# Gated DeltaNet in a hybrid layer: diagonal blocks of 16 by substitution on VectorE, and a second product buffer

## The reference

```python
h = rmsnorm(x, pre_norm)
proj = h @ w_in                      # 6.7k columns in three groups
# group a: gated DeltaNet, 4 heads of 128; group b: SSD, 16 heads; group c: retention, 4 heads
x = x + rmsnorm(concat(o_a, o_b, o_c) @ w_out, post_norm)
```

```python
a_low = einsum('bihd,bjhd->bhij', kb, ki) * decay * strict
sol = triangular_solve(a_low + eye, rhs, lower=True)     # then v_new = u - w @ S, and the state S moves on
```

## Time and profile before

| | us |
|---|---|
| median of three runs (2158.16 to 2159.24) | 2159.18 |
| the profiled execution's own time | 2162.2 |
| its span, first to last instruction | 2160.4 |
| PE busy, 14884 matmuls | 2080.1 |
| DVE busy | 1368.3 |
| ACT busy | 888.7 |
| POOL busy | 483.2 |

### The profile page before, as it was taken

One profiled execution on the slowest core, in us unless ns is written; L12 is line 12 of the kernel. 1 busy time (PEld: TensorE's weight loads), 2 busy tenths in 40 slices (PEclk: granted clock), 3 DMA queues, 4 the chain that ended last, 5 costly groups with the idle time before them and its releaser, 6 DMA issues.

```text
span 2160.4 us, 38435 instructions
## 1 busy us (share of the span) xinstructions
PE 2080.1 (96%) x14884; PEld 1918.3 (89%) x14884; DVE 1368.3 (63%) x3012; ACT 888.7 (41%) x1777; POOL 483.2 (22%) x432
## 2 busy tenths in 40 slices
PE   7899999999999999999999998999999999999996
PEld 6687889999898898999988898889988989999995
DVE  5678766646478876534577786774546787745333
ACT  5543366423343426511354445653325333652111
POOL 3433343322000112100333343432300010211000
PEclk9998999999999999999999999999999999999998
DMA  6653556667553455454575546667754343653442
GB/s 240 242 176 117 176 195 234 244 215 283 184 198 106 157 191 180 157 178 164 179 264 186 185 161 242 236 225 254 258 201 174 140 174 130 213 208 114 163 161 97
DMA packets 98196, 410.66 MB, mean 190 GB/s; under 512 B 11168, under 2 KB 12256, under 8 KB 84192
## 3 DMA queue, kind: packets, MB, share of 16 engines
q1 hardware_dynamic: 97440, 407.79, 53.8%
q10 hardware_dynamic: 576, 0.41, 0.1%
HBM read 257.00 MB, written 151.16 MB: 189 GB/s over the span
## 4 chain that ended last, share of the span: by engine, by line
PE 84%; issue 4%; DVE 4%; DMA 4%; ACT 2%; POOL 1%; SPq 0%; POOLq 0%; DVEq 0%; ACTq 0%
PE ps L1301 80%; PE ps L1304 4%; DMA wk<-cum_rows 1%; DMA wo_loaded<-in_w_out 1%; DMA wo_split<-wo_parts 1%; POOL w_low L2357 1%; DVE base L1795 1%; DMA w_split<-w_low 0%; ACT wk L2231 0%; DVE slot L1693 0%; DVE base L1794 0%; DMA wk<-in_x 0%; DMA w_loaded<-in_w_in 0%; DVE acc L2011 0%; DVE wk L1846 0%
## 5 line engine op out<-in xcount | busy, mean ns | idle before, releaser
L1301 PE MATMUL ps<-w_hi,hT_hi 128*128 128x256 f32 x1792 | 529.7, 296 | 11.8 <-POOL w_low L2357 10.0
L1301 PE MATMUL ps<-w_hi,hT_lo 128*128 128x256 f32 x1792 | 504.1, 281 | 0.0
L1301 PE MATMUL ps<-w_low,hT_hi 128*128 128x256 f32 x1792 | 502.9, 281 | 0.0
L2357 POOL TENSOR_TENSOR w_low<-w_loaded,w_hi 128x512 fp32r<-128x512 f32 x208 | 285.7, 1390 | 411.1 <-ACT w_hi L2074 411.0
L1301 PEld LDWEIGHTS ps<-w_hi,hT_hi 128*128 128x128 f32 x1792 | 338.9, 189 | 19.6 <-POOL w_low L2357 11.5
L1301 PEld LDWEIGHTS ps<-w_low,hT_hi 128*128 128x128 f32 x1792 | 339.3, 189 | 5.2 <-issue 4.8
L1301 PEld LDWEIGHTS ps<-w_hi,hT_lo 128*128 128x128 f32 x1792 | 340.2, 190 | 0.0
L1301 PE MATMUL ps<-hT_hi,w_hi 128*128 128x512 f32 x768 | 323.0, 421 | 9.4 <-POOL w_low L2357 9.4
L1301 PE MATMUL ps<-hT_lo,w_hi 128*128 128x512 f32 x768 | 304.2, 396 | 0.0
L1301 PE MATMUL ps<-hT_hi,w_low 128*128 128x512 f32 x768 | 303.8, 396 | 0.0
L1301 PE MATMUL ps<-wo_parts,mixT_hi 128*128 128x256 f32 x960 | 272.0, 283 | 0.0
(11 more groups left out here) (213 smaller groups left out, 3740.5 us busy)
## 6 DMA issues: line engine op xcount, KB each, us to landing
w_loaded<-in_w_in SPq DMA_DIRECT2D x104, 512.0 KB, 5.2
w_split<-w_hi SPq DMA_DIRECT2D x52, 1024.0 KB, 8.2
w_split<-w_low SPq DMA_DIRECT2D x52, 1024.0 KB, 10.1
w_hi<-w_split SPq DMA_DIRECT2D x104, 512.0 KB, 6.3
w_low<-w_split SPq DMA_DIRECT2D x104, 512.0 KB, 7.2
wo_loaded<-in_w_out SPq DMA_DIRECT2D x32, 512.0 KB, 4.4
wk<-cum_rows SPq DMA_DIRECT2D x32, 512.0 KB, 4.5
wo_split<-wo_parts SPq DMA_DIRECT2D x32, 512.0 KB, 8.6
```

The lines of the kernel that those rows point to most:

```text
L1301: return nc.tensor.matmul(o, a, b, start=start, stop=stop)
L2357: tt(w_lo[at], wr[at], w_hi[at], ALU.subtract)\
```

## The change

Blocks are 16 x 16 (`BASE` = 16), so `FIRST` is 4 and three levels are left; there are fifteen columns and sixteen row broadcasts. `COPIES` = 8 broadcasts are held at a time, in the head's own XT buffer: eight are made, four to a part, and used, then the other eight. Two product buffers `aTs` are used in turn by head parity; the new one is the spare quarter of slot 0, which tile 19 (the last half of sx 0) writes, so that half now waits for the last gdn_p of the third head. The base parts up to "spread" no longer touch X; "turn" waits for the last gdn_p of the preceding head. gdn_gram needs the last gdn_p of head h - 2 instead of h - 1. The pow of the norms on POOL is a step of its own, `gdn_rs`, placed after gdn_x0 of the preceding head. The order of pieces is new. The planner has new constants, and a rule by which an output unit isn't due before its load (`RELOAD`). The tail loads sort behind the unit loads released by the same step.

```diff
-BASE = 8
+BASE = 16
 FIRST = BASE.bit_length() - 1
+COPIES = 8
-PIECES = ([("gz", 0), ("gdn", 0), ("gdn", 1), ("gdn", 2), ("bc", 0), ("gz", 1), ("gdn", 3), ("bc", 1), ("gdn", 4), ("gdn", 5),
-           ("sx", 0, 0), ("sx", 0, 1), ("sz", 0, 0), ("sz", 0, 1), ("sx", 1, 0), ("sz", 1, 0), ("sx", 1, 1), ("sz", 1, 1)]
+PIECES = ([("gz", 0), ("gdn", 0), ("gdn", 1), ("gz", 1), ("bc", 0), ("gdn", 2), ("gdn", 3), ("bc", 1),
+           ("gdn", 4), ("sz", 0, 0), ("gdn", 5), ("sx", 0, 0), ("sx", 0, 1), ("sz", 0, 1), ("sx", 1, 0), ("sz", 1, 0),
+           ("sx", 1, 1), ("sz", 1, 1)]
...
 def base_parts():
-    copies = [("copy", range(i, min(i + 3, BASE))) for i in range(0, BASE, 3)]
-    columns = [("column", range(i, min(i + 2, BASE - 1))) for i in range(0, BASE - 1, 2)]
-    return [("mask", ()), ("sum", ()), *copies, *columns, ("spread", ()), ("turn", ())]
+    out = [("mask", ()), ("sum", ())]
+    for i in range(0, BASE, COPIES):
+        out += [("copy", range(j, min(j + 4, i + COPIES))) for j in range(i, i + COPIES, 4)]
+        out += [("column", range(j, min(j + 2, i + COPIES, BASE - 1))) for j in range(i, min(i + COPIES, BASE - 1), 2)]
+    return out + [("spread", ()), ("turn", ())]
...
+    if k == "gdn_turn":
+        return [("rs", ("gdn_rs", *step[1:]))]
...
+    def loaded_after():
+        return [("reload", order[-2])] if len(order) > 1 else []
...
-            return [("mixT", p, r[0], 2 * r[2] + 1), ("unit", out_no(step))]
+            return [("mixT", p, r[0], 2 * r[2] + 1), ("unit", out_no(step)), *(loaded_after() if p % 2 and r[2] == 0 and out_no(step) < TAIL else [])]
         if k == "split_out":
-            return [("raw", out_no(step)), ("kept", out_no(step) - 2)]
+            return [("raw", out_no(step)), ("kept", out_no(step) - 2), *loaded_after()]
...
-                "gdn_gram": lambda: ("gdn_p", p, r[0] - 1, LEVELS - 1, 1) if r[0] else None,
+                "gdn_gram": lambda: ("gdn_p", p, r[0] - 2, LEVELS - 1, 1) if r[0] > 1 else None,
+                "gdn_base": lambda: ("gdn_p", p, r[0] - 1, LEVELS - 1, 1) if r[0] and r[1] == BASE_END else None,
...
-LATE = 1000
+LATE = 200
-APART = 12
+APART = 16
-HOLD = 500
+RELOAD = 4400
+HOLD = 0
-AHEAD = 700
+AHEAD = 2000
-SLICE, LINE, TURN, UNIT, TABLE, MB = 705, 224, 109, 24 * 119, 1283, 3200
+SLICE, LINE, TURN, UNIT, TABLE, MB, LANDING = 705, 224, 109, 24 * 119, 1283, 3500, 2300
...
+    if PIECES[i] == ("sx", 0, N_SX - 1) and half == 1:
+        need += [("gdn_p", p, GH - 2, LEVELS - 1, j) for j in range(2)]
...
-        copies = [half.rearrange("p c n -> p (c n)").rearrange("p (j c n) -> p j c n", c=NT, n=BASE) for half in (X, more)]
-        copy_of = lambda j: copies[j // (P // BASE)][:, j % (P // BASE)]
+        aTs = (more, aT)
+        copy_of = lambda h, j: XTs[h % 2].rearrange("p c n -> p (c n)")[:, 0:COPIES * NT * BASE]\
+            .rearrange("p (j c n) -> p j c n", c=NT, n=BASE)[:, j % COPIES]
...
-                          u, ("tail", PARTS - 1, u)))
+                          len(units) + u, ("tail", PARTS - 1, u)))
...
                     if part == "mask":
                         wait_emptied(dve, ("gdn_gram", p, h))
-                        chain(tt(blocks(X), blocks(aT), own_block, ALU.mult))
+                        chain(tt(blocks(XTs[h % 2]), blocks(aTs[h % 2]), own_block, ALU.mult))
...
                     else:
+                        if h:
+                            for i in range(2):
+                                wait_filled(dve, ("gdn_p", p, h - 1, LEVELS - 1, i, "t"))
                         nc.vector.transpose(X.rearrange("p c n -> p (c n)"), XTs[h % 2].rearrange("p c n -> p (c n)")).then_inc(S["gdn_xt"], 1)
...
+                        if m == 19:
+                            for j in range(2):
+                                wait_filled(act, ("gdn_p", p, GH - 2, LEVELS - 1, j))
...
-                elif k == "gdn_turn":
+                elif k == "gdn_rs":
                     n = GH * p + s[2]
                     pool.wait_ge(S["gdn_sums"], n + 1)
```

More of the change, by code:

```diff
@@ L253, in dma @@
     def dma(work, *after):
-        return run("dma", work, *after) + 1700
+        return run("dma", work, *after) + LANDING
     def load_piece(n, after=()):
@@ L406, in play @@
                 load_piece(n + W_RING, ("n", ))
-                if n == PARTS * len(PIECES) - 1:
-                    for u in range(UNITS):
-                        at["unit", TAIL + u] = dma(MB, "n")
             elif p % 2 == 0:
@@ L446, in play @@
             mark("n", dve(900, "n"))
-            mark("rstd", pool(1640, "n"))
+            mark(("gdn_sums", p, r[0]), at["n"])
             mark(("kdc", p, r[0]), dve(640))
+        elif k == "gdn_rs":
+            mark(("rstd", p, r[0]), pool(1020, *after))
         elif k == "gdn_gram":
@@ L593, in make_plan @@
     done, smalls = {("small", -1)}, -1
-    sides = {k: [] for k in ("ssd", "fin", "norm", "post", "scale", "split", "unit")}
+    sides = {k: [] for k in ("ssd", "fin", "norm", "post", "scale", "split", "unit", "rs")}
     sides["unit"] += [("split_out", 0, 0, u) for u in range(2)]
@@ L626, in emit @@
                     at["emptied", tag] = clock["act" if emptied_by_act(step, tag) else "dve"] + 60
+        if (step == ("proj", PARTS - 1, len(PIECES) - 1, 1, Q - 1) or step == ("out", PARTS - 1, GROUPS - 2, UNITS - 3, NT // 2 - 1)) \
+                and ("proj", PARTS - 1, len(PIECES) - 1, 1, Q - 1) in done and ("out", PARTS - 1, GROUPS - 2, UNITS - 3, NT // 2 - 1) in done:
+            for u in range(UNITS):
+                at["tail"] = clock["pe"]
+                at["unit", TAIL + u] = dma(MB, "tail")
+        if step[0] == "small":
+            at["reload", step] = clock["pe"] + RELOAD
+        if step[0] == "out" and step[4] == NT // 2 - 1:
+            at["reload", step[:4]] = clock["pe"] + RELOAD
         if step[0] == "gdn_x0":
@@ L657, in known @@
                 "gdn_open": lambda: half_after(p, AT["gdn", (3 * r[0] + 2) // 2], (3 * r[0] + 2) % 2) if ("gdn_turn", p, r[0]) in done else ("gdn_turn", p, r[0]),
-                "gdn_x0": lambda: ("gdn_fin3", p, r[0] - 2) if r[0] > 1 else None,
+                "gdn_x0": lambda: ("gdn_fin3", p, r[0] - 2) if r[0] > 1 and ("gdn_rs", p, r[0]) in done else ("gdn_rs", p, r[0]),
+                "gdn_rs": lambda: ("gdn_x0", p, r[0] - 1) if r[0] else None,
                 "gdn_s": lambda: ("gdn_fin1", p, r[0] - 1) if r[0] and r[1] == 0 else None,
                 "gdn_v": lambda: ("gdn_xx", p, r[0], LEVELS - 1, r[1] // 2),
-                "gdn_gram": lambda: ("gdn_p", p, r[0] - 1, LEVELS - 1, 1) if r[0] else None,
+                "gdn_gram": lambda: ("gdn_p", p, r[0] - 2, LEVELS - 1, 1) if r[0] > 1 else None,
+                "gdn_base": lambda: ("gdn_p", p, r[0] - 1, LEVELS - 1, 1) if r[0] and r[1] == BASE_END else None,
                 "gdn_decay": lambda: ("cum_turn", p),
@@ L1256, in _ @@
                         wait_filled(sp, ("proj", PARTS - 1, len(PIECES) - 1 - v, 1))
[L1257 to L1260, removed]
+                    k = (GROUPS - 1) * UNITS + key[2]
+                    hi, lo = tail_parts(key[2])
+                    sp.dma_start(hi.bitcast(F32), wo_split[k, 0]).then_inc(tail_in[key[2]], 16)
+                    sp.dma_start(lo.bitcast(F32), wo_split[k, 1]).then_inc(tail_in[key[2]], 16)
                 else:
@@ L1769, in _ @@
                     for c in range(NT):
-                        ins = stt(aT[:, c, :], bank4(s)[:, c, :], own[:, 0, c:c + 1], et[:, h, c, :], ALU.mult, ALU.mult)
+                        ins = stt(aTs[h % 2][:, c, :], bank4(s)[:, c, :], own[:, 0, c:c + 1], et[:, h, c, :], ALU.mult, ALU.mult)
                     empty(ins, s)
@@ L1793, in _ @@
                             n = BASE - 1 - i
-                            chain(tt(step_t[:, :, i + 1:], copy_of(i)[:, :, i + 1:], cols_x[:, :, i:i + 1].broadcast_to([P, NT, n]), ALU.mult))
+                            chain(tt(step_t[:, :, i + 1:], copy_of(h, i)[:, :, i + 1:], cols_x[:, :, i:i + 1].broadcast_to([P, NT, n]), ALU.mult))
                             chain(tt(cols_x[:, :, i + 1:], cols_x[:, :, i + 1:], step_t[:, :, i + 1:], ALU.subtract))
```

11 lines of the change are left out of this document (7 added, 4 removed).

## The result

The changed kernel takes 2119.96 us (median of 4 runs, 2119.12 to 2121.73) where the kernel before took 2158.67 beside it: ratio 0.982, 95% interval 0.9805 to 0.9839, 38.7 us less. The forecast was 2108. The profiled execution took 2119.12 us, with a span of 2117.3 and a mean PE clock of 0.991.

A forecast was written before the change was run, and what follows sets the result against it. The prediction took PE, full in nearly all windows from 300 to 2090, to bound the kernel. Its terms, 28.7 + 12.7 + 12 + 4 - 6 = 51.4 us, gave 2108 us, with a range of 2078 to 2140.

The forecast's parts named there:

- level's matmuls: On PE, 256 matmul instructions of the removed level leave 16 heads at 112 ns each: 28.7 us less.
- tail: At the kernel's end, the unit's loads go ahead of the tail loads, ending PE's wait and half-clock restart: 12.7 us less.
- gaps of part 0: In the first part, earlier blocks and one more open piece let PE fill the state steps: 12 us less, bounds 0 and 27.
- planner numbers: Across the plan, new constants and the reload rule alter the order only: 4 us less, bounds 15 lost and 10 gained.
- DVE: 59 us more DVE work, mostly hidden by the second product buffer, delays level masks: 6 us lost, bounds 0 and 58.
- likeliest case: Whole kernel: the forecast of 2108 us, taken as 2092 to 2122; chance 0.52.
- the slot rule: First part: the front projection's next piece needs a slot freed by the next head's gdn_open, after the running head's last state step.
- rival 3: DeltaNet stages: base parts ahead of level masks make them DVE-paced, 34 us slower in all, 2193 us; chance 0.09.
- Rival 4: Whole kernel: PE isn't the bound, removed matmuls pay nothing and only the tail does, 2146 us; chance 0.05.
- Rival 1: Whole kernel: only PE's 28.7 us of work leaves, the tail gives little, DVE eats the rest, 2130 us; chance 0.20.

The follow-up runs named there:

- runs 1: Kernel before with tail loads sorted behind the unit loads the same step releases: 2148.21 us; changed kernel with the old sort key put back: 2129.06 us.
- runs 3: Changed kernel with blocks of 8, the level from 8 to 16 left out of the computation: 2096.81 us; with blocks of 8 and all four levels: 2133.49 us.
- runs 5: Changed kernel with the old piece order: 2146.07 us; with the old planner constants and reload time 0: 2161.66 us; with only AHEAD back at 700: 2155.05 us.
- run 7: Changed kernel with blocks of 8, all four levels, and piece order and waits chosen anew for that amount of work: 2110.26 us.
- run 2: Kernel before, blocks of 8 kept, with the level from 8 to 16 left out of the computation: 2138.51 us.

## Why the prediction was right, and where it was not

| term | predicted | measured | from |
|---|---|---|---|
| level's matmuls | -28.7 | -28.5 priced work | slack table |
| tail | -12.7 | -10.8 and -9.1 | runs 1 |
| gaps of part 0 | -12 | 0 (27.9 and 28.3 slack in 120 to 300; 8.5 without the larger blocks) | same prices, runs 3 |
| planner numbers | -4 | 42 lost when all are taken back, 35 with one | runs 5 |
| DVE | +6 | 23 regained without the larger blocks | runs 3 |
| sum | -51.4 | -38.7 | medians |

**The range held, the likeliest case too (2092 to 2122), but the sum is right in two terms only.** That 2120 lies within that case, 2 us from its edge, is in part luck: the gaps of part 0 gave nothing, and of the two smallest terms the planner numbers turned out worth far more than 4 and DVE far more than 6, with opposite signs. PE's priced work fell as the count said, and the tail load was read rightly from the queue. The tail paid 9 to 11 us in the runs, a little less than the 12.7; by priced slack the end is 14.7 us tighter, other reordering there included.

**Gaps of part 0 failed.** The step was: with head 1's block done early and one more piece open, PE fills the state steps. For head 1 that came true (46 matmuls in 15 us became 98 in 18). But the other half of it, that DVE has room for head 1's block chain beside head 0's steps, did not. From the timelines, the block chain from the start of the reduce to the start of the turn took 92.8 to 109.5, 139.7 to 155.0, 188.4 to 199.6 and 235.8 to 251.2 before, that is 17, 15, 11 and 15 us for the four heads. Now it takes 25, 26, 18 and 29 (86.7 to 111.6, 129.4 to 155.6, 183.7 to 202.2, 227.2 to 256.3). The prediction added 4.7 us to each; measured are 7 to 14, as the parts now stand on DVE among the levels and state steps of the head before. The saved level is eaten. The last state update of the four heads began at 156.6, 201.2, 253.5 and 281.6 before, and now at 163.5, 207.0, 261.5 and 285.5; in run 7 it begins at 153.0, 195.2, 233.9 and 260.7. That it is the larger blocks' DVE work which took the gain is shown by experiment 3: without it, and with the overlap and the order kept, the gaps closed by 20 us. The timeline of DVE, PE and POOL (start us, us) shows the sharing, a column of head 1 ahead of a state step of head 0:

```profile
145.90 0.20 DVE L1820 TENSOR_TENSOR base<-wk,base 128x40 f32<-128x40 f32 x1
146.12 1.26 POOL L2389 TENSOR_TENSOR w_low<-w_loaded,w_hi 128x512 fp32r<-128x512 f32 x1 [1.81 <-ACT w_hi L2103]
146.14 1.29 DVE L1821 TENSOR_TENSOR base<-base 128x40 f32<-128x40 f32 x1
147.47 0.35 DVE L1875 TENSOR_SCALAR wk<-ps,sc 128x128 f32<-128x128 f32 x1
...
148.07 1.19 PE L1327 MATMUL ps<-wk 128*128 128x128 f32 x4 [2.34 <-DVE wk L1875]
```

PE stood 2.34 us for an operation of 0.35. About 1.1 us of it is the subtract at 146.14, which took 1.29 us beside POOL's operation instead of 0.20.

**DVE was mis-sized in its effect, not in its work.** +59 us busy were predicted, +48 measured, with a column at 0.51 us of busy time (122.6 us over 240) where 0.50 was taken. I priced that work at 6 us because one window had DVE at 88% with PE full. That window stands in part 1 and it is still full (60.00 of 60). In part 0, where the slot rule ties PE to the chain of heads, DVE's work is paid. Taking out the larger blocks gave back 23 us for 85 of DVE, nearly all of it there; adding 48 that the plan did not know of cost 50, in all four stages. That is rival 3's mechanism, in the changed kernel in part 0 only, against gains that rival 3 didn't have. The Trainium skill ("VectorE: DVE Perf Modes", the TRN2 errata section) gives an fp32 tensor_tensor of N elements as (N+151)/0.96 ns, which for 60 elements makes an estimate of 220 ns. The two of them, with no POOL operation beside them, at 138.85 and 139.10 took 0.22 us each, so it agrees; over the kernel the mean of the form is 0.42.

**Planner numbers were the blind spot.** They were priced from PE's waits in the old plan. The runs show that order and constants are fitted to the amount of work: take one back and 26 to 42 us go, where the tail and the overlap are worth 9 to 11 each. So the terms don't add. The four reversals, each alone, sum to 9.1 + 9.5 + 26.1 + 41.7 = 86 us, twice the gain.

**What made the gain, then.** From the tail alone (2148.2) to blocks of 8 under the new order and overlap (2133.5) are 14.7 us, and blocks of 16 add 13.5 to that. Yet blocks of 8 under an order of their own reach 2110.3. The forecast that the level's matmuls come off the time is true only within one order; what the change gains can be had, and 10 us more, without the larger blocks. Rival 4 (PE isn't the bound) does not fit: the priced work fills 95% of both spans, and its fall makes 28.5 of the 43.1 us between them; in the kernel before, the level out paid 20.5 us (run 2), though there DVE lost 43 us as well. Rival 1 (2130) was as near in time as the forecast, and had part 0 right: its gaps stayed as large as before, which the prediction had named, with a time near 2130, as a sign of being wrong. It had the tail wrong, and neither saw the order.

**Open.** Whether an order exists in which blocks of 16 beat 2110: one try, of three waits and no other piece order, gave nothing. So blocks of 8 had the fuller choice, and that they are better in principle is not shown. If blocks of 16 had as little slack as the blocks of 8 have, they would be at 2110.3 - 28.5 = 2082, an estimate with no run behind it. Blocks of 8 without the level at 2096.8, under constants that aren't theirs, show that fewer matmuls are still worth time. How much of the 23 us between runs 3 (2133.5) and 7 (2110.3) is the piece order and how much the constants was not separated.

## What to carry to other kernels

Moving work from the bound engine to one at 63% is not free where the two share a chain: price it in the stage with the least room (here 90 to 285, DVE 79% busy before and 86% after), not in the best one. When the order of a kernel is planned from a cost model, retune the order for the kernel before as well, or the gain of the order is booked to the change; and don't read a single reverted constant as its worth. A load that PE needs next goes ahead of loads for later in the same queue: one sort key, 10 us.

## What the hardware showed that I had not expected

- Small DVE operations stretch beside POOL. The 40-element subtract above started 20 ns behind POOL's tensor_tensor and ended just after it, 1.29 us against 0.20 for its neighbour. The 28-element multiply took 215 ns in the mean before and 397 after, at the same width. In the changed kernel all 32 column operations that took over 0.4 us had a POOL instruction beside them, and of the 429 with none beside them the longest took 0.224 us. What stretches them was not tried apart.
- Shuffles of 64 elements issue 0.14 us apart (148.64, 148.78, 148.92) though each shows 0.22 busy: eight more and wider ones cost 1.5 us a head of summed busy time, less than the 2.0 taken.
- With the list fixed, DVE at 67% passed on 50.5 us for 47.9 put in: a share of busy time well under full said nothing of slack.
